# Expert sums and second-pass products of a decoder layer, alternated by four rows instead of eight, and a last block stored in halves

## The chip, the cores and the metric

The kernel runs on one core of a Trainium2 chip, all in fp32. The metric is the device time of one execution in microseconds (us). Its engines are PE (TensorE, matrix products into PSUM, which has 8 banks of 512 fp32 columns), DVE (VectorE), ACT (ScalarE), POOL (GpSimd, here only an issuer of transfers) and SP (another issuer). Transfers run on 16 DMA engines. Engines wait for one another through semaphores that the kernel sets by hand.

## The reference

One layer of a decoder for 512 prompt tokens and 8 sample tokens of width 1024:

```python
h  = rms_norm(x)*(1+sc1)+sh1            # adaLN: sh, sc, g come from c @ w_ada
q,k,v,p,ga,gb = split(h @ w_in)
A  = sliding_window_attention(q, k, v); B = multiscale_pool(p)
x  = x + g1*((sigmoid(ga)*(A@w_branch_attn) + sigmoid(gb)*(B@w_branch_pool)) @ w_out)
h2 = rms_norm(x)*(1+sc2)+sh2
x  = x + g2*PEER(h2)
```

PEER: for each of 8 heads a token's query (`h2 @ w_q`) is scored against two sets of 128 subkeys; the 16 best pairs name 16 of 16384 experts. Each expert is a row of `peer_u` and a row of `peer_v`, 1024 wide. The output is the sum over the 128 experts of a token of `gate * gelu(h2 . u_row) * v_row`.

## The kernel before

**Units.** The expert part works in 32 units (`UNITS`): block `b` of 128 tokens (four blocks) times one head. A unit has 16 U rows and 16 V rows; a "row" here is one indirect transfer by POOL (L543) that fetches one table row for each of the 128 tokens, 512 KB. A place of its own among the units, number 27 (`SAMPLES_AT`), serves the 8 sample tokens with 8 + 8 rows. That makes 520 U and 520 V gathers. U rows land in a ring of 6 buffers, V rows in another; from place 18 on (`MORE_UNIT`) each ring has 4 more.

**The order on POOL.** Its queue is written out by hand: for each place `p` and quarter `q` first four V rows of place `p - 2`, then four U rows of place `p`. A U gather waits until DVE has used the row that its buffer held (`u_used`), a V gather, at every second row, until PE has used the pair (`v_used`). What waits holds back all behind it.

**DVE** takes a dot product of each U row with the tokens (`dots`, L1121), scores and picks experts of later units between them (`route_unit`), and writes for each unit two sets of diagonal matrices (`coefficients`, L1135, `diag_ready`), eight rows each. **PE** adds the V rows into PSUM banks 0 to 3 (`combine`, L1531): a pair of rows takes 16 instructions of 64 x 64 tiles, and its end frees the pair (`v_used`). When the 8 units of a block are done, DVE scales the four banks with `g2` (`scale_sums`, L1149, `sums_scaled`), PE folds the halves and adds the transposed `x` (`fold`, L1557 and L1560, into banks 4 and 5), ACT copies the result to SBUF (`rows_out`, L740), and SP stores it (L493). Before a block's first sum PE waits until the four banks of the block before are scaled.

**Second pass.** The first part of the layer is computed for blocks 0 and 1 before the gathers begin; for blocks 2 and 3 and the sample tokens it is done beside the gathers, in steps `k` that all engines count alike: step `k` belongs to place `k // 4`, quarter `k % 4`. On PE that is `late_products(k)`: gate and A products in k = 8 to 15, gate and B in 16 to 23, the output product in 26 to 33, the transposed subkeys at 36, the mean square at 37, the token rows at `AT_H2N` (L1443), and from `AT_PQ` on one query product a step with its subkey scores (L1227, L1471, L1474). DVE (`late_work`) and ACT (`late_evacuations`) take the results; DVE normalizes at k = 39 (L854 to L870, then a memset at L1039 that raises `h_ready`), just before the scaling of block 0's sums at the start of place 10. These products use banks 4 to 7 in the order of `bank_plan`, in which the folded rows of block 0 stand as `("rows", 0, h)`. Their weights come by SP in chunks of 2 MB, in three buffers; a chunk is loaded once the last product from its buffer's chunk before is done.

PE's main loop runs over half places: two steps of products, then the eight V rows of half `f`.

```python
for n in range(2 * PLACES):
    p, f = n // 2 + 2, n % 2
    for k in (2 * n + 8, 2 * n + 9):
        late_products(k)
    ...
    combine(unit_at(p - 2), f)
    if n % 16 == 1 and 16 < n < 56:
        fold(n // 16 - 1)
```

Of the kernel before, what the change touches and what calls it, by code (L numbers as in the profile page):

```python
# [40 lines left out]
PH = 8  # L41
# [11 lines left out]
MORE_UNIT = 18  # L53
SAMPLES_AT = 27
PLACES = UNITS + 1
AT_A, AT_B, AT_O2, AT_SK, AT_SS, AT_MEAN, AT_NORM, AT_H2N, AT_PQ = 8, 16, 26, 36, 37, 38, 39, 41, 42
HW = 64


# [52 lines left out]
def bank_plan():  # L112
# [52 lines left out]
    for m in range(17):  # L165
        plan += [(("pq", m, 1), "A")] if m < 16 else []
        for i in score_tiles(m):
            plan += [(("sc", i, 1), "A"), (("scs", i), "A")]
        if m == 1:
            plan += [(("rows", 0, h), "A") for h in both]  # L170
    return plan

# [37 lines left out]
def decoder_layer(nc, x_prompt, x_sample, cache_k, cache_v, state_pool, c_prompt, c_sample, norm1_g,  # L210
# [204 lines left out]
    def unit_at(p):  # L415
        return p if p < SAMPLES_AT else p - 1
# [24 lines left out]
    def _(sp):  # L441
# [46 lines left out]
        for b in range(NB):  # L488
            if b == NB - 1:
                sp.wait_ge(sample_y_ready, 1)  # L490
                sp.dma_start(y_sample[:, 0, :], g2s_rows[0:S, :]).then_inc(sample_y_stored, 16)
            sp.wait_ge(y_ready, b + 1)
            sp.dma_start(y_prompt[0, b * P:(b + 1) * P, :], y_rows).then_inc(y_stored, 16)  # L493
        sp.wait_ge(y_stored, 16 * NB)
        sp.wait_ge(sample_y_stored, 16)

    def slot_rounds(i):
# [88 lines left out]
    def _(act):  # L586
# [143 lines left out]
        def rows_out(b):  # L730
            out = y_rows.rearrange("p (a b) -> p a b", a=2)
            if b == 0:
                for h in range(2):
                    copy(("rows", 0, h), out[:, h, :], bank(("rows", 0, h)))
                act.wait_ge(emptied_by_act, turn[("rows", 0, 1)])
                act.nop().then_inc(y_ready, 1)
                return
            act.wait_ge(rows_folded, b)
            act.wait_ge(y_stored, 16 * b)
            act.activation(out, psum[:, 4:6, :], ACT.Copy).then_inc(y_ready, 1)  # L740

        def query_scores(m, h):
            if 2 <= m < 16:
# [81 lines left out]
    def _(dve):  # L825
# [316 lines left out]
        def scale_sums(b):  # L1142

            dve.wait_ge(v_used, row(PH * b + PH - 1, TOPK))
            if b:
                dve.wait_ge(y_ready, b)
            for i in range(4):
                h = slice(i % 2 * 512, (i % 2 + 1) * 512)
                dve.tensor_tensor(scaled[i], psum[:, i, :].rearrange("p (a b) -> p a b", a=2), g2b[:, h].rearrange("p (a b) -> p a b", a=2), ALU.mult).then_inc(sums_scaled, 1)  # L1149

# [58 lines left out]
    def _(pe):  # L1209
# [300 lines left out]
            if AT_PQ <= k <= AT_PQ + 16:  # L1510
                query_scores(k - AT_PQ, 1)

        def combine(u, f):
            b, n = u // PH, 2 * u + f
            if n % 16 == 0:
                if b:
                    pe.wait_ge(sums_scaled, 4 * b)
                else:
                    for i in range(4):
                        wait_emptied(pe, plan[max(j for j in range(len(plan)) if bank_of[j] == i)][0])  # L1520
            pe.wait_ge(diag_ready, n + 1)
            for k in range(0, 8, 2):
                first, last = n % 16 == 0 and k == 0, n % 16 == 15 and k == 6
                pair = [row(u, 8 * f + k + i) for i in range(2)]
                for r in pair:
                    pe.wait_ge(v_landed[v_buf[r]], v_landing[r])
                for h in range(2):
                    for g in range(2):
                        ps = slice(g * HW, (g + 1) * HW)
                        for i, r in enumerate(pair):  # L1530
                            ins = pe.matmul(psum[i * HW:(i + 1) * HW, 2 * g + h, :], diags[n % 4][ps, k + i, :],  # L1531
                                            v_rows[v_buf[r]][ps, h * 512:(h + 1) * 512],
                                            start=first, stop=last, skip_group_check=True)
                ins.then_inc(v_used, 2)

        def combine_samples(f):
            pe.wait_ge(sample_coef_ready, 1)
            pe.wait_ge(sample_h_used, 2 * S)
            for t in range(4 * f, 4 * f + 4):
                r = sample_row(t)  # L1540
                pe.wait_ge(v_landed[v_buf[r]], v_landing[r])
                for h in range(2):
                    ins = pe.matmul(psum[0:S, 6 + h, :], coef_s[:, t * S:(t + 1) * S], v_rows[v_buf[r]][:, h * 512:(h + 1) * 512],
                                    start=(t == 0), stop=(t == S - 1), skip_group_check=True)
                ins.then_inc(v_used, 1)
            if f:
                pe.wait_ge(v_used, sample_row(S))
                pe.nop().then_inc(sample_out_ready, 2)

        def fold(b):  # L1550
            pe.wait_ge(sums_scaled, 4 * (b + 1))
            if b > 1:
                pe.wait_ge(y_ready, b)
            for h in range(2):
                o = begin(("rows", 0, h)) if b == 0 else psum[:, 4 + h, :]
                for g in range(2):
                    pe.matmul(o.rearrange("p (a b) -> p a b", a=2), halves_on[:, (1 - g) * HW:(3 - g) * HW], scaled[2 * g + h],  # L1557
                              start=(g == 0), stop=False, skip_group_check=True)
                for c in range(4):
                    ins = pe.matmul(o[:, c * P:(c + 1) * P], xT[:, 4 * h + c, cols(b)], ident,  # L1560
                                    start=False, stop=(c == 3), skip_group_check=True)
                if b == 0:
                    end(ins)
            if b:
                ins.then_inc(rows_folded, 1)

        def pick_rows(first, end_t):
            for t in range(first, end_t):
# [5 lines left out]
                    pe.matmul(psum[:, 6 + h, :], pick_s[:, t, :], h2n[NB][:, h * 512:(h + 1) * 512],  # L1574
                              start=True, stop=True).then_inc(sample_h_ready, 1)

        for n in range(2 * PLACES):
            p, f = n // 2 + 2, n % 2
            for k in (2 * n + 8, 2 * n + 9):
                late_products(k)  # L1580
            if 2 * n + 8 == AT_PQ + 18:
                for key, _ in plan[-BANKS:]:
                    wait_emptied(pe, key)
            if (p, f) == (SAMPLES_AT - 1, 1):
                pick_rows(0, 4)
            if (p, f) == (SAMPLES_AT, 1):
                pick_rows(4, S)
            if p - 2 == SAMPLES_AT:
                combine_samples(f)
            else:  # L1590
                combine(unit_at(p - 2), f)
            if n % 16 == 1 and 16 < n < 56:
                fold(n // 16 - 1)
            if (p, f) == (23, 1):
                pe.wait_ge(sample_spread, 2)
                for i in range(2):
                    ins = pe.matmul(psum[:, 6, i * S:(i + 1) * S], hs_spread[0:PH * S, i, :], kc[0:PH * S, K_SEQ:K_SEQ + S], start=True, stop=True)
                ins.then_inc(sample_turned, 1)
            if (p, f) == (SAMPLES_AT - 2, 0):
                pe.wait_ge(sample_routed, 1)  # L1600
                for i, (src, first) in enumerate(((xT, T), (mods[:, 40:48, :], 1))):
                    if i:
# [34 lines left out]
```

## Time and profile before

| | us |
|---|---|
| median of 3 runs (lowest, highest) | 1910.24 (1908.02, 1910.49) |
| the profiled execution: its own time | 1913.8 |
| its span, first to last instruction | 1911.9 |
| PE busy | 1327.0 (69%) |
| DVE busy | 1108.7 (58%) |
| POOL busy | 1108.0 (58%) |
| ACT busy | 258.6 (14%) |

The page of the profile gives busy time by engine, then 40 slices of the span, the transfers by queue, and the chain of work that ended last. A busy PE is not a PE at its peak: its clock has two levels and the page's mean granted clock is 0.82 of the full one. In views of windows, "DMA share" is the mean busy share of the 16 DMA engines; it can read a little over 1. In timelines, the bracket behind an instruction is the idle time of its engine in front of it and what ended that.

### The profile page before, as it was taken

To read this page: it belongs to the slowest core of one execution; us is meant where nothing else is said; L and a number is where in the kernel's file an instruction comes from. 1 tells how busy PE (TensorE), PEld (TensorE's weight loads), DVE (VectorE), ACT (ScalarE), POOL (GpSimd) and SP (SyncE) were. 2 spreads that over 40 slices of the span, in tenths; PEclk is the share of its full clock that TensorE was granted. 3 is DMA by queue.
4 is the path that set the end of the run, shared out by engine and by line. 5 is a ranking of instruction groups with operands and counts; after the bars stand their busy time and mean duration, and the time that the engine had idled before them with its cause. 6 is when DMAs were issued, how large, how long until landed. Compare 5 with 4: busy or idle time off the path is not lost.

```text
span 1911.9 us, 19507 instructions
## 1 busy us (share of the span) xinstructions
PE 1327.0 (69%) x7067; PEld 672.8 (35%) x7067; DVE 1108.7 (58%) x2613; ACT 258.6 (14%) x489; POOL 1108.0 (58%) x1066
## 2 busy tenths in 40 slices
PE   5999899896778857645877655556555547764567
PEld 3547667585344423213444211111111112211122
DVE  5013331267656667767557667767777666686540
ACT  2114430221111100111111101000000011100000
POOL 1201000036766677765677777777777777777773
PEclk8999897798799978788889876676667788777769
DMA  9334143869999999997999999999999999999996
GB/s 329 109 100 148 60 137 110 306 244 318 374 372 403 373 399 405 400 404 277 387 371 379 389 408 397 400 377 404 355 407 407 406 405 408 408 370 362 388 409 268
DMA packets 196265, 639.21 MB, mean 334 GB/s; under 512 B 21856, under 2 KB 23188, under 8 KB 196042
## 3 DMA queue, kind: packets, MB, share of 16 engines
q0 software_dynamic: 154992, 550.65, 74.6%
q1 hardware_dynamic: 41178, 87.31, 13.1%
q8 instruction: 57, 0.93, 0.2%
q14 instruction: 38, 0.31, 0.0%
HBM read 634.09 MB, written 3.59 MB: 334 GB/s over the span
## 4 chain that ended last, share of the span: by engine, by line
POOL 36%; PE 30%; DMA 15%; issue 12%; DVE 4%; ACT 2%; SPq 0%; DVEq 0%; POOLq 0%; ACTq 0%
POOL arena L543 36%; PE psum L1227 12%; DMA arena<-in_peer_v,arena 10%; PE psum L1531 7%; PE psum L1291 5%; DMA arena<-in_peer_u,arena 3%; PE psum L1245 1%; ACT arena L591 1%; DVE arena L1121 1%; DMA arena<-in_w_ada 1%; ACT arena L643 1%; PE psum L1318 1%; DMA arena<-in_w_in 1%; PE psum L1557 0%; DMA arena<-in_x_sample 0%
## 5 line engine op out<-in xcount | busy, mean ns | idle before, releaser
L1531 PE MATMUL psum<-arena 64*64 64x512 f32 x4096 | 665.9, 800 | 489.3 <-DMA arena<-in_peer_v,arena 474.6
L1121 DVE CUSTOM_DVE_ANT_0 arena<-arena 128x1024 f32<-128x1024 f32 x520 | 635.1, 1227 | 431.1 <-DMA arena<-in_peer_u,arena 413.4
L543 POOL DMA_INDIRECT arena<-in_peer_v,arena x520 | 548.3, 1054 | 228.2 <-issue 145.0
L543 POOL DMA_INDIRECT arena<-in_peer_u,arena x520 | 533.9, 1027 | 227.7 <-issue 155.4
L1531 PEld LDWEIGHTS psum<-arena 64*64 64x64 f32 x4096 | 202.6, 179 | 931.3 <-issue 914.2
L1227 PE MATMUL psum<-arena 128*128 128x264 f32 (+3 forms) x1620 | 382.7, 394 | 15.3 <-ACT arena L591 15.0
L1227 PEld LDWEIGHTS psum<-arena 128*128 128x128 f32 (+1 forms) x1620 | 304.2, 194 | 92.3 <-issue 41.7
L591 ACT ACTIVATE arena<-psum 128x512 f32<-128x512 f32 (+9 forms) x219 | 91.7, 447 | 492.1 <-PE psum L1227 281.1
L728 ACT ACTIVATE arena<-arena 128x16 f32<-128x16 f32 x32 | 6.9, 217 | 836.6 <-DVE arena L1121 836.6
L1291 PE MATMUL psum<-arena 128*128 128x512 f32 (+3 forms) x240 | 88.5, 528 | 2.9 <-DMA arena<-in_w_in 2.9
L1291 PEld LDWEIGHTS psum<-arena 128*128 128x128 f32 (+1 forms) x240 | 40.7, 172 | 49.9 <-issue 42.9
L538 POOL DMA_DIRECT2D arena<-in_cache_v x1 | 0.5, 537 | 87.6 <-PE psum L1401 87.6
L540 POOL DMA_DIRECT2D arena<-in_consts x1 | 0.6, 589 | 78.3 <-PE psum L1436 78.3
L1121 DVE DVE_READ_ACCUMULATOR2_ANT arena<- 128x1 f32 x520 | 43.0, 83 | 0.0
L1135 DVE TENSOR_TENSOR arena<-arena 128x512 f32<-128x512 f32 x64 | 41.6, 691 | 1.1
L728 ACT ACT_TABLE_LOAD x32 | 41.1, 1283 | 0.2
L726 ACT ACT_TABLE_LOAD x31 | 39.8, 1283 | 0.5
L1046 DVE MAX8 arena<-arena 128x8 f32<-128x128 f32 (+3 forms) x99 | 29.8, 329 | 17.1 <-ACT arena L591 16.9
L523 POOL DMA_DIRECT2D arena<-arena x2 | 1.1, 544 | 61.8 <-DVE arena L911 61.8
L848 DVE TENSOR_TENSOR arena<-psum,arena 128x36 f32<-128x36 f32 x12 | 2.3, 195 | 59.5 <-PE psum L1253 59.5
L922 DVE SCALAR_TENSOR_TENSOR arena<-psum,arena 128x512 f32<-128x512 f32 (+1 forms) x16 | 9.4, 622 | 46.8 <-PE psum L1318 46.7
L1245 PE MATMUL psum<-arena 128*32 128x512 f32 x192 | 29.8, 752 | 8.5 <-DMA arena<-in_w_ada 8.5
(197 smaller groups left out, 852.0 us busy)
## 6 DMA issues: line engine op xcount, KB each, us to landing
arena<-in_w_ada SPq DMA_DIRECT2D x12, 2048.0 KB, 12.3
arena<-in_w_in SPq DMA_DIRECT2D x10, 2048.0 KB, 14.6
arena<-in_peer_wq SPq DMA_DIRECT2D x8, 2048.0 KB, 14.2
arena<-in_peer_u,arena POOLq DMA_INDIRECT x520, 6.6
arena<-in_peer_v,arena POOLq DMA_INDIRECT x520, 7.1
arena<-in_w_out SPq DMA_DIRECT2D x4, 2048.0 KB, 14.2
arena<-in_w_branch_attn SPq DMA_DIRECT2D x4, 1024.0 KB, 11.4
arena<-in_w_branch_pool SPq DMA_DIRECT2D x2, 2048.0 KB, 12.0
```

The costliest lines, as they stand in the source:

```text
L543: pool.indirect_dma_start(out=rows_to, out_offset=None, in_=table[0], in_offset=bass.IndirectOffsetOnAxis(ap=index, axis=0)).then_inc(land ...
L591: ins = act.activation(out, in_, f, **kw)
L643: act.activation(sS[b % 2][:, h, lo:], sS[b % 2][:, h, lo:], ACT.Exp, bias=nmax[:, h:h + 1], accum_out=ssum[:, h:h + 1])
L726: act.activation(v, v, ACT.Exp)
L728: act.activation(acts[:, u % 2, :], acts[:, u % 2, :], ACT.Gelu_apprx_tanh).then_inc(gelu_done, 1)
L1046: dve.max(v[:, 0:8], s)
L1121: dve.tensor_tensor_reduce(rows_r, rows_r, h, 1.0, 0.0, ALU.mult, ALU.add, total).then_inc(u_used, 1)
L1135: dve.tensor_tensor(diags[n % 4], halves_on[:, HW:2 * HW].unsqueeze(1).broadcast_to((P, 8, HW)), coefs[:, 8 * f:8 * f + 8].unsqueeze(2).br ...
L1227: ins = pe.matmul(out, a, b, start=(n == 0), stop=(n == len(pairs) - 1))
L1245: ins = pe.matmul(o[k % 4 * 32:(k % 4 + 1) * 32, :], scT[:, k, :], w[:, k, :], start=(k < 4), stop=(k >= 4), skip_group_check=True)
L1291: ins = pe.matmul(o, hT[:, k, cols(b)], wt[:, k, 0:n], start=(k == 0), stop=(k == C - 1))
L1531: ins = pe.matmul(psum[i * HW:(i + 1) * HW, 2 * g + h, :], diags[n % 4][ps, k + i, :], v_rows[v_buf[r]][ps, h * 512:(h + 1) * 512], start= ...
```

## The change

Five things change; the amount of arithmetic does not.

- PE's loop runs over steps `k`: one step of products, then four V rows of quarter `q` (before: two steps, then eight rows). What hung on a half place hangs on a quarter; the sample rows go two by two.
- The token rows move from step 41 to 42, the query products from 42 on to 43 on. The folded rows of block 0 keep their step, 43, so that they stand one query product earlier in the order of banks.
- DVE scales the four banks in the order 0, 2, 1, 3: both parts of the first column half, then both of the second.
- A fold first adds the transposed `x` to both column halves, and only then waits for the scaled sums, half by half.
- ACT copies the folded rows in halves, and for the last block each half is stored by a transfer of its own.

```diff
--- before.py
+++ after.py
@@ -53,7 +53,7 @@
 MORE_UNIT = 18
 SAMPLES_AT = 27
 PLACES = UNITS + 1
-AT_A, AT_B, AT_O2, AT_SK, AT_SS, AT_MEAN, AT_NORM, AT_H2N, AT_PQ = 8, 16, 26, 36, 37, 38, 39, 41, 42
+AT_A, AT_B, AT_O2, AT_SK, AT_SS, AT_MEAN, AT_NORM, AT_H2N, AT_PQ = 8, 16, 26, 36, 37, 38, 39, 42, 43
 HW = 64
 
 
@@ -166,7 +166,7 @@
         plan += [(("pq", m, 1), "A")] if m < 16 else []
         for i in score_tiles(m):
             plan += [(("sc", i, 1), "A"), (("scs", i), "A")]
-        if m == 1:
+        if AT_PQ + m == 43:
             plan += [(("rows", 0, h), "A") for h in both]
     return plan
 
@@ -489,9 +489,14 @@
             if b == NB - 1:
                 sp.wait_ge(sample_y_ready, 1)
                 sp.dma_start(y_sample[:, 0, :], g2s_rows[0:S, :]).then_inc(sample_y_stored, 16)
-            sp.wait_ge(y_ready, b + 1)
-            sp.dma_start(y_prompt[0, b * P:(b + 1) * P, :], y_rows).then_inc(y_stored, 16)
-        sp.wait_ge(y_stored, 16 * NB)
+            if b < NB - 1:
+                sp.wait_ge(y_ready, b + 1)
+                sp.dma_start(y_prompt[0, b * P:(b + 1) * P, :], y_rows).then_inc(y_stored, 16)
+        for h in range(2):
+            hs = slice(h * 512, (h + 1) * 512)
+            sp.wait_ge(y_ready, NB + h)
+            sp.dma_start(y_prompt[0, T - P:, hs], y_rows[:, hs]).then_inc(y_stored, 16)
+        sp.wait_ge(y_stored, 16 * (NB + 1))
         sp.wait_ge(sample_y_stored, 16)
 
     def slot_rounds(i):
@@ -735,9 +740,12 @@
                 act.wait_ge(emptied_by_act, turn[("rows", 0, 1)])
                 act.nop().then_inc(y_ready, 1)
                 return
-            act.wait_ge(rows_folded, b)
             act.wait_ge(y_stored, 16 * b)
-            act.activation(out, psum[:, 4:6, :], ACT.Copy).then_inc(y_ready, 1)
+            for h in range(2):
+                act.wait_ge(rows_folded, 2 * b - 1 + h)
+                ins = act.activation(out[:, h, :], psum[:, 4 + h, :], ACT.Copy)
+                if h or b == NB - 1:
+                    ins.then_inc(y_ready, 1)
 
         def query_scores(m, h):
             if 2 <= m < 16:
@@ -1144,7 +1152,7 @@
             dve.wait_ge(v_used, row(PH * b + PH - 1, TOPK))
             if b:
                 dve.wait_ge(y_ready, b)
-            for i in range(4):
+            for i in (0, 2, 1, 3):
                 h = slice(i % 2 * 512, (i % 2 + 1) * 512)
                 dve.tensor_tensor(scaled[i], psum[:, i, :].rearrange("p (a b) -> p a b", a=2), g2b[:, h].rearrange("p (a b) -> p a b", a=2), ALU.mult).then_inc(sums_scaled, 1)
 
@@ -1510,59 +1518,60 @@
             if AT_PQ <= k <= AT_PQ + 16:
                 query_scores(k - AT_PQ, 1)
 
-        def combine(u, f):
-            b, n = u // PH, 2 * u + f
-            if n % 16 == 0:
+        def combine(u, q):
+            b, n, v = u // PH, 2 * u + q // 2, 4 * u + q
+            if v % 32 == 0:
                 if b:
                     pe.wait_ge(sums_scaled, 4 * b)
                 else:
                     for i in range(4):
                         wait_emptied(pe, plan[max(j for j in range(len(plan)) if bank_of[j] == i)][0])
             pe.wait_ge(diag_ready, n + 1)
-            for k in range(0, 8, 2):
-                first, last = n % 16 == 0 and k == 0, n % 16 == 15 and k == 6
-                pair = [row(u, 8 * f + k + i) for i in range(2)]
+            for k in (0, 2):
+                first, last = v % 32 == 0 and k == 0, v % 32 == 31 and k == 2
+                pair = [row(u, GS * q + k + i) for i in range(2)]
                 for r in pair:
                     pe.wait_ge(v_landed[v_buf[r]], v_landing[r])
                 for h in range(2):
                     for g in range(2):
                         ps = slice(g * HW, (g + 1) * HW)
                         for i, r in enumerate(pair):
-                            ins = pe.matmul(psum[i * HW:(i + 1) * HW, 2 * g + h, :], diags[n % 4][ps, k + i, :],
+                            ins = pe.matmul(psum[i * HW:(i + 1) * HW, 2 * g + h, :], diags[n % 4][ps, q % 2 * GS + k + i, :],
                                             v_rows[v_buf[r]][ps, h * 512:(h + 1) * 512],
                                             start=first, stop=last, skip_group_check=True)
                 ins.then_inc(v_used, 2)
 
-        def combine_samples(f):
+        def combine_samples(q):
             pe.wait_ge(sample_coef_ready, 1)
             pe.wait_ge(sample_h_used, 2 * S)
-            for t in range(4 * f, 4 * f + 4):
+            for t in (2 * q, 2 * q + 1):
                 r = sample_row(t)
                 pe.wait_ge(v_landed[v_buf[r]], v_landing[r])
                 for h in range(2):
                     ins = pe.matmul(psum[0:S, 6 + h, :], coef_s[:, t * S:(t + 1) * S], v_rows[v_buf[r]][:, h * 512:(h + 1) * 512],
                                     start=(t == 0), stop=(t == S - 1), skip_group_check=True)
                 ins.then_inc(v_used, 1)
-            if f:
+            if q == 3:
                 pe.wait_ge(v_used, sample_row(S))
                 pe.nop().then_inc(sample_out_ready, 2)
 
         def fold(b):
-            pe.wait_ge(sums_scaled, 4 * (b + 1))
             if b > 1:
                 pe.wait_ge(y_ready, b)
+            o = [begin(("rows", 0, h)) if b == 0 else psum[:, 4 + h, :] for h in range(2)]
             for h in range(2):
-                o = begin(("rows", 0, h)) if b == 0 else psum[:, 4 + h, :]
+                for c in range(4):
+                    pe.matmul(o[h][:, c * P:(c + 1) * P], xT[:, 4 * h + c, cols(b)], ident,
+                              start=(c == 0), stop=False, skip_group_check=True)
+            for h in range(2):
+                pe.wait_ge(sums_scaled, 4 * b + 2 * h + 2)
                 for g in range(2):
-                    pe.matmul(o.rearrange("p (a b) -> p a b", a=2), halves_on[:, (1 - g) * HW:(3 - g) * HW], scaled[2 * g + h],
-                              start=(g == 0), stop=False, skip_group_check=True)
-                for c in range(4):
-                    ins = pe.matmul(o[:, c * P:(c + 1) * P], xT[:, 4 * h + c, cols(b)], ident,
-                                    start=False, stop=(c == 3), skip_group_check=True)
+                    ins = pe.matmul(o[h].rearrange("p (a b) -> p a b", a=2), halves_on[:, (1 - g) * HW:(3 - g) * HW], scaled[2 * g + h],
+                                    start=False, stop=(g == 1), skip_group_check=True)
                 if b == 0:
                     end(ins)
-            if b:
-                ins.then_inc(rows_folded, 1)
+                else:
+                    ins.then_inc(rows_folded, 1)
 
         def pick_rows(first, end_t):
             for t in range(first, end_t):
@@ -1574,29 +1583,28 @@
                     pe.matmul(psum[:, 6 + h, :], pick_s[:, t, :], h2n[NB][:, h * 512:(h + 1) * 512],
                               start=True, stop=True).then_inc(sample_h_ready, 1)
 
-        for n in range(2 * PLACES):
-            p, f = n // 2 + 2, n % 2
-            for k in (2 * n + 8, 2 * n + 9):
-                late_products(k)
-            if 2 * n + 8 == AT_PQ + 18:
+        for k in range(8, 4 * PLACES + 8):
+            p, q = divmod(k, 4)
+            late_products(k)
+            if k == AT_PQ + 18:
                 for key, _ in plan[-BANKS:]:
                     wait_emptied(pe, key)
-            if (p, f) == (SAMPLES_AT - 1, 1):
+            if (p, q) == (SAMPLES_AT - 1, 2):
                 pick_rows(0, 4)
-            if (p, f) == (SAMPLES_AT, 1):
+            if (p, q) == (SAMPLES_AT, 2):
                 pick_rows(4, S)
             if p - 2 == SAMPLES_AT:
-                combine_samples(f)
+                combine_samples(q)
             else:
-                combine(unit_at(p - 2), f)
-            if n % 16 == 1 and 16 < n < 56:
-                fold(n // 16 - 1)
-            if (p, f) == (23, 1):
+                combine(unit_at(p - 2), q)
+            if q == 3 and p % PH == 2 and PH < p < 28:
+                fold(p // PH - 1)
+            if (p, q) == (23, 3):
                 pe.wait_ge(sample_spread, 2)
                 for i in range(2):
                     ins = pe.matmul(psum[:, 6, i * S:(i + 1) * S], hs_spread[0:PH * S, i, :], kc[0:PH * S, K_SEQ:K_SEQ + S], start=True, stop=True)
                 ins.then_inc(sample_turned, 1)
-            if (p, f) == (SAMPLES_AT - 2, 0):
+            if (p, q) == (SAMPLES_AT - 2, 0):
                 pe.wait_ge(sample_routed, 1)
                 for i, (src, first) in enumerate(((xT, T), (mods[:, 40:48, :], 1))):
                     if i:
```

## Rows read from the trace of the kernel before

**Rows 1.** The page: the chain by line, and the transfers by queue.

```profile
POOL arena L543 36%; PE psum L1227 12%; DMA arena<-in_peer_v,arena 10%; PE psum L1531 7%; PE psum L1291 5%; DMA arena<-in_peer_u,arena 3%; PE psum L1245 1%; ACT arena L591 1%; DVE arena L1121 1%; DMA arena<-in_w_ada 1%; ACT arena L643 1%; PE psum L1318 1%; DMA arena<-in_w_in 1%; PE psum L1557 0%; DMA arena<-in_x_sample 0%
...
q0 software_dynamic: 154992, 550.65, 74.6%
```

**Rows 2.** Windows by stage: length, busy us by engine, PE clock, DMA share, GB/s.

```profile
470.00:660.00 190.00, 143.46 (x779) 82.04 (x780) 122.41 (x298) 20.41 (x33) 130.81 (x123) 0.87 0.99 379
660.00:855.00 195.00, 122.69 (x709) 53.79 (x711) 135.08 (x336) 19.70 (x32) 139.53 (x136) 0.80 1.03 402
855.00:905.00 50.00, 28.28 (x188) 15.80 (x180) 35.87 (x84) 10.79 (x19) 28.48 (x27) 0.82 0.76 284
905.00:1080.00 175.00, 137.07 (x794) 75.66 (x798) 108.71 (x265) 23.02 (x55) 124.26 (x120) 0.88 0.99 378
```

**Rows 3.** Waits of PE and POOL, 470 to 860 us: total, times, longest.

```profile
PE psum L1531 <- DMA arena<-in_peer_v,arena: 118.0, 27, 12.0
...
POOL arena L543 <- PE psum L1531: 42.5, 20, 5.8
```

**Rows 4.** Timeline of PE and POOL: start, length, instructions, idle time before.

```profile
495.80 10.96 PE L1227 MATMUL psum<-arena 128*128 128x264 f32 x48
...
539.89 1.95 PE L1531 MATMUL psum<-arena 64*64 64x512 f32 x16 [2.42 <-DMA arena<-in_peer_v,arena]
...
627.26 10.96 PE L1227 MATMUL psum<-arena 128*128 128x264 f32 x48
638.15 3.67 PE L1531 MATMUL psum<-arena 64*64 64x512 f32 x32
...
640.40 0.97 POOL L543 DMA_INDIRECT arena<-in_peer_v,arena  x1 [5.32 <-PE psum L1531]
...
673.74 3.69 PE L1531 MATMUL psum<-arena 64*64 64x512 f32 x16 [3.90 <-DMA arena<-in_peer_v,arena]
```

**Rows 5.** Windows around three of POOL's stalls (columns as in rows 2).

```profile
536.00:542.00 6.00, 3.42 (x32) 0.91 (x24) 5.71 (x19) 0.00 (x0) 4.81 (x4) 1.00 0.79 262
638.00:650.00 12.00, 8.85 (x66) 2.59 (x65) 7.16 (x23) 0.00 (x0) 7.47 (x8) 0.90 0.81 278
...
953.00:966.00 13.00, 8.77 (x65) 2.60 (x64) 6.53 (x16) 3.16 (x5) 8.61 (x8) 0.83 0.80 267
```

**Rows 6.** Timeline at the second normalization: DVE, PE and POOL.

```profile
873.91 2.43 DVE L1149 TENSOR_TENSOR arena<-psum,arena 128x512 f32<-128x512 f32 x4
...
874.06 5.38 PE L1443 MATMUL psum<-arena 128*128 128x128 f32 x24 [16.22 <-DVE arena L1039]
...
879.37 5.55 PE L1531 MATMUL psum<-arena 64*64 64x512 f32 x48
...
881.79 1.21 POOL L543 DMA_INDIRECT arena<-in_peer_v,arena  x1 [13.90 <-PE psum L1531]
```

**Rows 7.** Timeline of the query steps: fold 0 on PE, and a stall of POOL.

```profile
914.91 1.99 PE L1557 MATMUL psum<-arena 128*128 128x512 f32 x4
...
955.25 1.78 POOL L543 DMA_INDIRECT arena<-in_peer_v,arena  x1 [4.75 <-PE psum L1531]
```

**Rows 8.** Timeline of the tail, all engines.

```profile
1898.34 2.49 DVE L1149 TENSOR_TENSOR arena<-psum,arena 128x512 f32<-128x512 f32 x4 [39.57 <-PE psum L1531]
...
1900.88 3.39 PE L1557 MATMUL psum<-arena 128*128 128x512 f32 x4 [2.60 <-DVE arena L1149]
...
1904.11 1.05 PE L1560 MATMUL psum<-arena 128*128 128x128 f32 x8
...
1905.00 1.88 PE L1557 MATMUL psum<-arena 128*128 128x512 f32 x4
...
1907.81 1.03 ACT L740 ACTIVATE arena<-psum 128x1024 f32<-128x1024 f32 x1 [51.05 <-PE psum L1560]
1908.87 0.35 SPq L493 DMA_DIRECT2D out<-arena  x1
```

**Rows 9.** Transfers issued in 555 to 600 us: count, size, us to landing.

```profile
arena<-in_w_branch_pool SPq DMA_DIRECT2D x1, 2048.0 KB, 14.7
```

## The prediction

> **What bounds the kernel now.** I read the page's chain first, then the transfers, then windows by stage, then single waits. The chain that ended last is 36% POOL and 15% DMA: it runs through the gathers of L543 [rows 1]. Their queue moves 550.65 MB in 1040 gathers, so 0.529 MB each. In 660–855 us the 16 DMA engines show a share of 1.03 at 402 GB/s, which is what this kernel reaches when they never pause; in 470–660 the share is 0.99, in 855–905 it is 0.76, in 905–1080 it is 0.99 [rows 2]. Time in which nothing moved is length × (1 − share/1.03): 190 × 0.039 = 7.4 us, 50 × 0.262 = 13.1 us, 175 × 0.039 = 6.8 us. So from the first gather on the transfers are the limit, and a change of order on PE can win only these pauses, 27.3 us together, and the tail after the last gather.
>
> Who makes the pauses? PE waits 118.0 us for second-pass rows between 470 and 860, so it has time to spare on average; yet POOL waits 42.5 us in 20 waits for PE in the same stretch [rows 3]. Both hold because of bursts: PE does two steps of products (48 matmuls, 10.96 us), then eight V rows, of which the first two pairs, already there, take 3.67 us [rows 4]. While it multiplies it frees no V buffer; there are six, POOL's queue is in order, and so the U gathers wait too. At 640.40 POOL had stood 5.32 us until the sums behind the products of 627.26 freed a pair [rows 4]. Around that stall the DMA share is 0.81 over 12 us, around another of the kind 0.79 over 6 us [rows 5]. Elsewhere in this stretch the same stall is covered by weights in flight.
>
> **The change, part by part.** The sum is made against the profiled execution, 1913.8 us (span 1911.9 us and 1.9 us around it); the median of the runs shown is 1910.24 us, 3.56 us less, and I carry the gain over to it.
>
> *Alternating by one step and four rows.* No instruction is added; 5.48 us of products (10.96/2) and 3.67 us of sums now follow each other, 9.15 us a step. A step takes (627.26 − 495.80)/10 = 13.1 us [rows 4], so PE keeps its slack, and the longest stretch without freeing a buffer halves. A stall of 5.32 us at 10.96 us of products is covered at 5.48 us. Gain at 470–660: at least 0, at most 7.4 us (all of its pauses). I take the two pauses that are visibly this stall, 6 × (1 − 0.79/1.03) + 12 × (1 − 0.81/1.03) = 1.4 + 2.6 = 4.0 us [rows 5]. The same stall at 955.25 (4.75 us of POOL, [rows 7]) has a share of 0.80 over 13 us [rows 5]: 2.9 us, bounds 0 and the stage's 6.8 us. In 660–855 there is no pause to win: 0, and since nothing pauses there, at worst a stall like the 5.32 us above. A product of an odd step now stands behind four V rows, up to 3.67 us and their landing later; DVE, which takes it, waited in 470–860 for nothing but rows (no wait on PE stands in its waits there), and POOL's order brings it those rows after PE's; I take 0, at worst 3.67 us at one place.
>
> One weight chunk gets less time: `wb` is loaded into the buffer of `wa`, free when the last A product (k = 15) is done, and needed one step later. It landed 14.7 us after its issue [rows 9]; PE now comes to it after four rows and a gate product, as little as 3.67 + 3.65 = 7.3 us later (the gate product is 16 of the 48 matmuls, 10.96/3), so PE may stand up to 7.4 us once. During that the transfers are busy with that very chunk: price 0, at worst 7.4 − 5.48 = 1.9 us.
>
> *Query products and token rows one step later.* This moves the token-row transposes (L1443) behind the first four rows of unit 8. Now PE stands until the second normalization is done, transposes 5.38 us from 874.06, and only at 879.37 adds the rows that free a buffer; POOL, idle for 13.90 us, goes on at 881.79 [rows 6]. DVE's four scalings end at 873.91 + 2.43 = 876.34, and these are all that the rows of unit 8 need. After the change the first pair runs from 876.34. At the lower clock it takes 3.69 us as after 3.90 us of waiting, at the upper 1.95 us as after 2.42 us [rows 4]. POOL goes on at 880.0 or 878.3, so 1.8 or 3.5 us earlier. PE has stood for 16.2 us there (idle in front of L1443), so the nearest row is the lower clock: 1.8 us. Nothing is won below 0, as the scalings come after the normalization on DVE anyway. The transposes move into the wait for the next gathered rows. The step that follows fold 0 waits for ACT's copies of the folded rows in the banks it reuses; before, a later step did so. Price 0, at worst as the 4.75 us stall.
>
> *Tail.* The last V sum ends near 1898.3; four scalings take 2.49 us; then PE folds: 3.39 + 1.05 + 1.88 + 1.05 us with gaps, ACT copies 1.03 us from 1907.81, and the store is issued at 1908.87 [rows 8]. After: the transposes of x (2 × 1.05 us) stand in front of the wait and run beside the scalings, to 1900.4. Two scalings, now those of the first half, are done at 1899.6, the others at 1900.83. The first half folds to 1902.3 and the second to 1904.2 (1.88 us each), its copy is half as wide (I take 0.6 us for 1.03), so the last store is issued at 1904.85 instead of 1908.87: 4.0 us. PE no longer stands in front of the fold, as in fold 0, where the same four matmuls took 1.99 us [rows 7], not the 3.39 us after the idle time of [rows 8]. The store of 512 KB ran from 1908.87 to the span's end, 3.0 us; half the bytes save at most half, at least 0: I take 0.5 us. Tail: 4.5 us; at the lower clock for one half 1.5 us less, so 3.0 to 5.5.
>
> The Trainium skill (DMA: Bandwidth & Descriptors, Anatomy of one DMA) gives each transfer about 2.0 us that do not depend on size, plus bytes at 436 GB/s. By it, as an estimate, 256 KB saves 0.6 us of a store's 3.2 us, near the 3.0 us of the trace; if the two halves paid their fixed part one after the other, the tail would win 2.5 us.
>
> *Sum:* 4.0 + 2.9 + 1.8 + 4.5 = 13.2 us, so 1900.6 us for an execution such as the profiled one and 1910.24 − 13.2 = **1897.0 us**.
>
> **Rivals.**
> 1. *The transfers hide it* (16%). POOL's stalls go, but the pauses come back at another gather, since a gather costs POOL 1.25 us with its gap and the transfers 0.529 MB/402 GB/s = 1.32 us: a lost backlog is regained by 0.07 us per gather only. For it: most stalls of POOL now cost no transfer time. Against: four measured pauses stand right behind a stall. Left is the tail: 1905.7 us (1904.7 to 1907.2).
> 2. *All goes* (12%): every pause of 470–660 and 905–1080, the upper clock at unit 8, the whole tail: 7.4 + 6.8 + 3.5 + 4.7 = 22.4 us, 1887.8 us.
> 3. *Slower by the change of array shape* (5%). Products use the array whole (128*128), sums in quarters (64*64). The change doubles the passages between them: some 23 pairs of steps are split, 46 more passages. In the rows none is to be seen: sums start at 638.15, 0.07 us before the modelled end of the products (627.26 + 10.96) [rows 4]. The place is each of the 43 steps; it decides from (13.1 − 9.15)/2 = 2.0 us a passage, when a step no longer fits. At 2.5 us a passage, the steps cost 43 × 1 = 43 us and nothing but the tail is won: 1949 us. The Trainium skill (TensorEngine Tiling (Array Packing), Key Properties) says that changing the tiling mode drains the engine, and names no price; by it this is what speaks against the change, and these rows show none.
> 4. *Slower by the clock* (4%). The granted clock is 0.87 in 470–660 [rows 2]. If shorter bursts left PE at the lower of its two levels (1.2 instead of 2.4 GHz) for over 43% of a step's work (13.1/9.15 − 1), PE would be the limit; at 60% a step costs 1.5 us, 43 steps 66 us: 1910.2 − 4.5 + 66 = 1972 us. Against: the waits get shorter, and pairs after short waits ran at the upper level [rows 4].
> 5. *Half done* (3%): the late `wb`, the copies behind fold 0 and a displaced stall take 1.9 + 4.75 + 5.32 = 12.0 us of it back: 1909 us.
>
> **How the numbers follow.** The forecast has 60%, with its own range of 1892 to 1903 us; the rivals 16, 12, 5, 4 and 3%. About 0.2% (3.8 us) can be told from no change here. Faster by more: 60 + 12 + 10 of rival 1 = 82%. Within: 6 of rival 1 and rival 5, 9%. Slower: 9%. The range from rival 2 to the poor end of rival 1, 1887.5 to 1907.2 us, leaves out rivals 3 to 5, 12%, and some of the edges.
>
> **What would show it.** Right: POOL's waits for L1531 in 470–860 fall from 42.5 us to under 15; the share in 470–660 and 905–1080 rises to 1.01 or more; POOL's stop at the normalization shrinks from 13.90 to about 12 us; from the last V sum to the last store's issue 6.5 us instead of 10.5, with no PE wait over 0.3 us in front of the fold. Wrong: POOL's waits gone but the shares unchanged (rival 1); gaps of PE at each passage (rival 3); a granted clock under 0.75 in 470–660 (rival 4); a wait of PE on a weight chunk at k = 16 or for ACT after fold 0 (rival 5).

## The result and the profile after

Before and after ran in turn on one chip: 1909.33 us before (median of 4), 1886.54 us after (1883.07 to 1887.77), ratio 0.9875 with a 95% interval of 0.986 to 0.9891. That is 22.8 us, where 13.2 were forecast; the time lies below the stated range by 1 us. In two later groups, beside other runs of before, the ratio was 0.989 (0.9861 to 0.9919) and 0.9867 (0.9839 to 0.9895), and the medians were 21.0 and 23.6 us apart.

The windows by stage of the kernel after, columns as in [rows 2]:

```profile
470.00:660.00 190.00, 154.38 (x872) 89.10 (x872) 127.28 (x307) 23.42 (x36) 138.63 (x129) 0.91 1.02 394
660.00:855.00 195.00, 114.87 (x662) 49.95 (x658) 134.32 (x335) 19.27 (x31) 143.00 (x133) 0.81 1.02 399
855.00:905.00 50.00, 29.39 (x188) 14.31 (x189) 36.13 (x86) 6.32 (x10) 29.28 (x29) 0.80 0.79 295
905.00:1080.00 175.00, 138.30 (x845) 76.65 (x847) 114.61 (x279) 27.66 (x65) 131.64 (x128) 0.94 1.02 403
```

Read the last column against [rows 2]: 379 became 394 GB/s in 470–660 and 378 became 403 in the query steps. The clock rose too (0.87 to 0.91, 0.88 to 0.94). The share beside it rose only from 0.99 to 1.02: 3%, where the rate rose by 4.0 and 6.6%. The same microseconds hold slightly different work in two kernels, so stages are compared between the same gathers further down.

Four rows from the timeline of PE show the new alternation, to be read beside [rows 4]: 5.6 us of products, then each pair as it lands, after 1.25 and 1.46 us of waiting. The products run as fast as before, 5.61 us for 24 matmuls where 48 took 10.96 us.

```profile
502.41 5.61 PE L1235 MATMUL psum<-arena 128*128 128x264 f32 x24
509.28 1.95 PE L1539 MATMUL psum<-arena 64*64 64x512 f32 x16 [1.25 <-DMA arena<-in_peer_v,arena]
512.68 1.95 PE L1539 MATMUL psum<-arena 64*64 64x512 f32 x16 [1.46 <-DMA arena<-in_peer_v,arena]
514.56 5.61 PE L1235 MATMUL psum<-arena 128*128 128x264 f32 x24
```

POOL's waits for PE in 470–860 (total, times, longest), against 42.5 us in [rows 3]:

```profile
POOL arena L548 <- PE psum L1539: 30.9, 23, 5.3
```

The longest is the one that the prediction placed: PE waits for the late `wb` chunk at step 16.

```profile
561.58 3.83 PE L1235 MATMUL psum<-arena 128*128 128x264 f32 x16
571.53 3.59 PE L1235 MATMUL psum<-arena 128*128 128x264 f32 x8 [6.12 <-DMA arena<-in_w_branch_pool]
...
577.30 0.94 POOL L548 DMA_INDIRECT arena<-in_peer_v,arena  x1 [5.34 <-PE psum L1539]
```

It cost no transfer time: neither the window over PE's wait nor the one over POOL's wait behind it falls below a share of 1.02 or 402 GB/s.

```profile
562.00:572.00 10.00, 3.88 (x17) 3.03 (x16) 5.58 (x14) 1.89 (x3) 7.83 (x8) 0.79 1.02 404
572.00:582.00 10.00, 9.49 (x52) 5.41 (x52) 3.07 (x7) 0.00 (x0) 3.78 (x4) 0.87 1.03 402
```

The second normalization, against [rows 6]: it starts at 854.84 (L862), the first sums of unit 8 follow DVE's scaling behind it, the token rows (L1451) come later, and POOL's stop is 12.50 instead of 13.90 us.

```profile
854.84 1.80 DVE L862 RECIPROCAL arena<-arena 128x264 f32<-128x264 f32 x1
...
863.61 2.42 DVE L1157 TENSOR_TENSOR arena<-psum,arena 128x512 f32<-128x512 f32 x4
866.08 8.12 PE L1539 MATMUL psum<-arena 64*64 64x512 f32 x48 [17.16 <-DVE arena L1157]
870.07 1.34 POOL L548 DMA_INDIRECT arena<-in_peer_v,arena  x1 [12.50 <-PE psum L1539]
...
879.88 3.80 PE L1451 MATMUL psum<-arena 128*128 128x128 f32 x24
```

The tail, against [rows 8]: the 16 transposes of x follow the last sums at once, beside the scaling, and the fold runs at the upper clock (3.60 us for eight matmuls). ACT ends at 1883.21, 6.05 us after the end of the last V sum (1875.21 + 1.95); before, with the last V sum in the row below, it was 10.55 us.

```profile
1896.34 1.95 PE L1531 MATMUL psum<-arena 64*64 64x512 f32 x16 [0.55 <-DMA arena<-in_peer_v,arena]
```

After:

```profile
1875.21 1.95 PE L1539 MATMUL psum<-arena 64*64 64x512 f32 x16 [0.54 <-DMA arena<-in_peer_v,arena]
...
1877.09 2.05 PE L1564 MATMUL psum<-arena 128*128 128x128 f32 x16
1877.22 2.48 DVE L1157 TENSOR_TENSOR arena<-psum,arena 128x512 f32<-128x512 f32 x4 [40.31 <-PE psum L1539]
...
1878.98 3.60 PE L1569 MATMUL psum<-arena 128*128 128x512 f32 x8
...
1880.96 0.60 ACT L746 ACTIVATE arena<-psum 128x512 f32<-128x512 f32 x1 [46.05 <-PE psum L1569]
...
1881.58 1.99 SPq L498 DMA_DIRECT2D out<-arena  x2
...
1882.61 0.60 ACT L746 ACTIVATE arena<-psum 128x512 f32<-128x512 f32 x1 [1.06 <-PE psum L1569]
```

The first gather starts anywhere from 393 to 404 us in the profiles of this study, whether or not a kernel is changed there. So stages are compared below by the starts of gathers in each trace: the first gather, then the first V gather in the turn of places 2, 10, 11, 15 and 19 (gathers 33, 289, 321, 449, 577), the last gather, the end of the span. Lengths in us, one profile each; "tail" runs from the start of the last gather to the end, and the 70 to 72 us ahead of place 2 stand in the last column alone:

```
kernel                 places 2-10  10-11  11-15  15-19  19-last  tail  first gather to end
before                    384.2      57.5  187.2  171.7   617.0   23.8     1511.1
after                     378.2      54.9  176.8  174.1   616.5   18.4     1488.3
after, second group       375.7      53.5  177.1  173.8   616.6   18.9     1485.7
after, third group        376.4      55.9  179.7  175.4   607.6   18.0     1482.5
e1 loop only              379.4      55.9  176.5  172.8   613.7   22.0     1490.6
e2 shift only             388.1      55.3  192.1  171.8   611.1   21.8     1510.0
e3 tail only              389.6      55.5  188.5  172.0   612.5   18.9     1505.9
e5 bursts to step 37      386.4      53.1  179.0  174.6   615.4   18.3     1495.8
e6 bursts from step 42    378.5      55.3  193.2  172.3   609.3   18.9     1497.3
e7 loop and tail          378.9      54.3  178.0  171.2   617.5   19.2     1489.3
e4 normalization later    376.4      48.3  176.5  173.6   615.4   17.9     1478.9
e9 the same again         377.5      48.2  177.9  173.3   614.2   18.8     1480.1
e8 pairs                  376.6      50.2  179.8  174.4   614.0   18.0     1482.9
```

### The profile page after: what moved, and what is told of

The parts are those of the page before. It is cut to its first block, busy times and chain, and to the rows that moved or that the text cites. A ratio compares the mean times of both kernels' runs of the same rounds, so it can differ in the third digit from the quotient of the medians.

```text
span 1885.7 us, 19511 instructions
## 1 busy us (share of the span) xinstructions
PE 1301.2 (69%) x7067; PEld 661.3 (35%) x7067; DVE 1108.4 (59%) x2613; ACT 257.9 (14%) x492; POOL 1113.2 (59%) x1066
## 3 DMA queue, kind: packets, MB, share of 16 engines
q1 hardware_dynamic: 41322, 87.31, 13.2%
## 4 chain that ended last, share of the span: by engine, by line
POOL 42%; PE 23%; DMA 16%; issue 14%; DVE 3%; ACT 2%; SPq 0%; DVEq 0%; POOLq 0%; ACTq 0%
POOL arena L548 42%; DMA arena<-in_peer_v,arena 11%; PE psum L1235 8%; PE psum L1539 5%; PE psum L1299 5%; DMA arena<-in_peer_u,arena 3%; ACT arena L596 1%; PE psum L1253 1%; DMA arena<-in_w_ada 1%; DMA arena<-in_w_in 1%; DVE arena L1129 1%; ACT arena L648 1%; PE psum L1326 1%; DMA arena<-in_x_sample 0%; PE psum L1583 0%
## 5 line engine op out<-in xcount | busy, mean ns | idle before, releaser
L1539 PE MATMUL psum<-arena 64*64 64x512 f32 x4096 | 647.6, 776 | 504.2 <-DMA arena<-in_peer_v,arena 454.6
L548 POOL DMA_INDIRECT arena<-in_peer_u,arena x520 | 541.2, 1041 | 223.3 <-issue 155.1
L596 ACT ACTIVATE arena<-psum 128x256 f32<-128x256 f32 (+9 forms) x219 | 90.8, 447 | 528.1 <-PE psum L1235 317.9
## 6 DMA issues: line engine op xcount, KB each, us to landing
arena<-in_w_in SPq DMA_DIRECT2D x10, 2048.0 KB, 13.6
```

What stands on the lines that cost most here:

```text
L548: pool.indirect_dma_start(out=rows_to, out_offset=None, in_=table[0], in_offset=bass.IndirectOffsetOnAxis(ap=index, axis=0)).then_inc(land ...
L596: ins = act.activation(out, in_, f, **kw)
```

## The experiments

Theory A: PE's bursts of two steps starve the V buffers, and what that costs is read from the transfer rate. Rival B: the query steps gain because they stand one step later. The first group splits the change into its parts and adds one new edit.

**e1, the loop alone** (in short, against the kernel before).

```diff
-        for n in range(2 * PLACES):        # two steps, then combine(u, f): eight rows
+        for k in range(8, 4 * PLACES + 8): # one step, then combine(u, q): four rows
```

> Of the change only the loop of one step and four V rows; steps 41 and 42 stay for token rows and query products, fold, scaling order and store are as before. Theory A (PE's bursts of two steps starve the V buffers, and the loss is what the transfer rate shows, not the pauses in the DMA share): the loop carries about 7 us in steps 8 to 33 and about 10 us in the query steps, so 15 to 18 us faster than before; GB/s in 470-660 about 394 and in the query steps about 400. Rival B (the query steps gain because query products and token rows stand one step later): 6 to 9 us faster, GB/s in the query steps still under 385.

Measured: 1886.59 us against 1907.98 us before, ratio 0.988 (0.9845 to 0.9915). The rates are those of the whole change; windows 470–660 and 905–1080:

```profile
470.00:660.00 190.00, 156.61 (x872) 89.52 (x872) 125.58 (x304) 23.41 (x36) 138.08 (x129) 0.91 1.01 394
905.00:1080.00 175.00, 130.98 (x817) 72.00 (x819) 113.57 (x275) 25.55 (x59) 127.97 (x127) 0.93 1.02 405
```

The gain, 21 us by medians, is over A's 15 to 18, though the interval (16 to 30 us) reaches into it. B falls: without the shift the query steps reach 405 GB/s.

**e2, the shift alone** (in short; the folded rows and the last wait for the banks are set to match).

```diff
-AT_H2N, AT_PQ = 41, 42
+AT_H2N, AT_PQ = 42, 43
```

> Of the change only token rows and query products one step later, in the old loop of two steps and eight rows. Theory A: at most 3 us faster (the stop at the normalization), or no difference that can be told; the query steps stay under 385 GB/s. Rival B: 8 to 12 us faster.

Measured: ratio 1.0026 (0.9999 to 1.0052), nothing that can be told from no change. The query steps are as slow as before:

```profile
905.00:1080.00 175.00, 134.12 (x796) 74.73 (x800) 106.70 (x262) 23.48 (x57) 126.61 (x116) 0.89 0.98 371
```

**e3, the tail alone** (in short).

```diff
-            for i in range(4):         # scale_sums
+            for i in (0, 2, 1, 3):
-            act.activation(out, psum[:, 4:6, :], ACT.Copy)
+            for h in range(2): act.activation(out[:, h, :], psum[:, 4 + h, :], ACT.Copy)
 ...                                    # fold: x first; SP: two stores for the last block
```

> Of the change only the fold with the transposed x first, the scaling order and the last block stored in halves. Both theories: 4.5 to 5.5 us faster, all of it behind the last gather; 10.5 us from the last V sum to the last store's issue become about 6.

Measured: 1903.83 us, ratio 0.9971 (0.9944 to 0.9998), 4.2 us by medians. Behind the last gather it has 18.9 us where before has 23.8: 4.9 us. But e1 and e2, which have the old tail, have 22.0 and 21.8 us there; see the tail below.

**e4, the whole change with the normalization behind the scaling.** The rows above show PE waiting 17.16 us for DVE, which normalizes (step 39) and only then scales block 0's sums.

```diff
-AT_NORM, AT_H2N, AT_PQ = 39, 42, 43
+AT_NORM, AT_H2N, AT_PQ = 40, 42, 43
```

> The whole change, and the second normalization one step later (40 for 39), so that DVE scales block 0's sums before it normalizes and PE's first sums of unit 8 no longer wait for the normalization. If POOL's stop of 12.5 us there is PE waiting for DVE's scaling: the stop falls under 5 us and the kernel is 4 to 9 us faster than the whole change (1878 to 1883 us). If DVE's time for the normalization (8.9 us) is what counts, since it holds up the dot products as well, the stop moves to the U buffers and the time stays within 2 us of the whole change.

Measured: 1881.85 us, ratio 0.9861 (0.9824 to 0.9898); the whole change did not run in this group. POOL's stop is 3.83 us, and DVE's reciprocal (L862), the start of the normalization, stands behind the scaling:

```profile
857.71 2.48 DVE L1157 TENSOR_TENSOR arena<-psum,arena 128x512 f32<-128x512 f32 x4
...
860.24 8.05 PE L1539 MATMUL psum<-arena 64*64 64x512 f32 x48 [7.87 <-DVE arena L1157]
...
864.23 1.48 POOL L548 DMA_INDIRECT arena<-in_peer_v,arena  x1 [3.83 <-PE psum L1539]
...
868.47 1.80 DVE L862 RECIPROCAL arena<-arena 128x264 f32<-128x264 f32 x1
```

The second group puts the bursts back in one stage at a time, and takes the shift out.

> The whole change, unaltered, beside the others of this group: 1883 to 1888 us; its profile from the first gather to the end 1488 us, as before.

Measured: 1887.73 us, ratio 0.989, and 1485.7 us from the first gather.

**e5 and e6, bursts in one stage.** The whole change, with

```diff
+            if k < 38:                 # e5; e6: if k >= 42
+                for i in (k, k + 1) if q % 2 == 0 else ():
+                    late_products(i)
+            else:
                 late_products(k)
```

> The whole change, but up to step 37 PE does two steps of products ahead of eight V rows again. Theory A (each stage gains the transfer rate that its own bursts cost): 5 to 8 us slower than the whole change, GB/s in 470-660 back to 378 to 385, in the query steps still about 403. If the gain of the query steps comes from a backlog that the early steps build, the query steps fall as well and it is over 12 us slower.

> The whole change, but from step 42 on PE does two steps ahead of eight V rows again. Theory A: 8 to 13 us slower than the whole change, GB/s in the query steps back to 375 to 382, in 470-660 still about 394. By the terms of the prediction, read from pauses in the DMA share, it would be 3 us slower.

Measured: e5 1896.2 us, ratio 0.9937 (0.9917 to 0.9957), 8.5 us over the whole change in its group by medians; e6 1900.74 us, ratio 0.9945 (0.9926 to 0.9965), 13.0 us over it by medians (10.5 by the ratios). e5's interval just touches that of the whole change, e6's does not; e5 lies a little over A's 5 to 8 us, e6 at the upper end of its 8 to 13. Each loses in its own stage (table) and keeps the rate of the other. First e5, then e6, windows 470–660 and 905–1080:

```profile
470.00:660.00 190.00, 148.13 (x816) 84.50 (x816) 123.48 (x299) 23.23 (x36) 128.29 (x120) 0.88 0.99 380
905.00:1080.00 175.00, 139.03 (x856) 78.46 (x848) 115.59 (x275) 27.47 (x65) 129.65 (x125) 0.96 1.02 399
```

```profile
470.00:660.00 190.00, 148.66 (x826) 85.51 (x827) 126.86 (x307) 20.24 (x32) 138.95 (x127) 0.89 1.01 393
905.00:1080.00 175.00, 138.08 (x792) 75.87 (x796) 105.39 (x255) 23.98 (x57) 121.32 (x114) 0.86 0.97 367
```

A rival that these rows answer is the clock, which rose with the rate: in 470–660 e5 and e6 have nearly the same clock, 0.88 and 0.89, but 380 and 393 GB/s. There the rate goes with the bursts.

**e7, loop and tail without the shift** (the diff of e2 the other way round).

> The whole change without its shift of token rows and query products (41 and 42 as before). If the shift is worth the 1.8 us of the prediction: 2 us slower than the whole change. If it costs, as the sum of the single parts suggests (loop 20.6, shift 1.1, tail 5.2 us from the first gather on, against 22.7 for all): 2 to 4 us faster than the whole change.

Measured: 1883.55 us, ratio 0.987 (0.9844 to 0.9896), beside 0.989 (0.9861 to 0.9919) for the whole change: the medians say 4 us faster, the intervals overlap. That the shift gains is not shown; that it costs isn't either. In the table the kernels with the shift and single steps after it have 173 to 175 us in places 15 to 19, the others 171 to 173; why is open.

The third group sets e4's edit beside the whole change, and alternates more finely still.

> The whole change, unaltered, as the base of the two others: 1883 to 1889 us.

> The whole change with the normalization at step 40, again, beside the whole change on one chip: 4 to 8 us faster than it, all of it between the first gathers of places 10 and 11 (48 us instead of 54).

Measured: 1887.03 us for the whole change, 1879.84 us with the normalization later, ratio 0.983 (0.9803 to 0.9856) to before. The median is 7.2 us lower, places 10 to 11 take 48.2 instead of 55.9 us. The intervals of whole change and e9 still overlap, but five of the six runs of the whole change in this group are slower than all six of e9.

**e8, pairs** (e9's kernel, in short). In steps 8 to 23 PE does the gate product, one pair of rows, the A or B product, one pair.

```diff
-            late_products(k)
+            late_products(k, (0,)); combine(unit, q, (0,)); late_products(k, (1,))
 ...
-                combine(unit, q)
+                combine(unit, q, (2,))
```

> The whole change with the normalization at step 40, and in steps 8 to 23 a finer alternation: the gate product, one pair of V rows, the second product, one pair. Theory A with the V buffers as the limit: a burst of 5.5 us is already covered, so within 3 us of the kernel without it (e9). If every burst costs in proportion, 470-660 rises from 394 to 402 GB/s and it is 3 to 4 us faster than e9. Either way the passages between array shapes double again: at 0.4 us each they would show as 25 us of PE time, and as slower.

Measured: 1877.78 us, ratio 0.982 (0.9792 to 0.9848), not told from e9; 470–660 is at 396 GB/s, e9's at 398. Halving bursts of 5.5 us gains nothing more that can be told, and twice the passages between array shapes in these steps cost nothing that can be seen.

## Why the prediction was wrong

The mechanism was right: bursts on PE hold up POOL, and with it the transfers (e1, e5, e6). Two terms of the sum were less than a half and about a quarter of what they measured. The step that failed is the first one: "Time in which nothing moved is length × (1 − share/1.03)", and with it the choice of "the two pauses that are visibly this stall" as the gain. The same rows hold a second measure, the rate: 190 × (1 − 379/402) = 10.9 us and 175 × (1 − 378/402) = 10.4 us are missing, not 7.4 and 6.8, and what the alternation gave back is about that, not only the three dips of [rows 5].

- *Steps 8 to 36*: 4.0 us forecast. Places 2 to 10 take 384 to 390 us in the four profiles with bursts there, 376 to 379 us in the nine without: 9.6 us between the means; e5 says 8.5 by medians. The stated upper bound of 7.4 us was too low as well.
- *Query steps*: 2.9 us forecast, upper bound 6.8. Places 11 to 15 take 187 to 193 us with bursts and 176 to 180 without: about 12 us; e6 says 10 to 13. This is the term that missed most.
- *Normalization*: 1.8 us forecast, 1.4 us of POOL's stop measured (13.90 to 12.50), with the first pair at the lower clock as taken. But it is not the shift's alone. With one step at a time the four rows of step 40 stand ahead of the token rows at 41 anyway. Each part by itself shortens the stop as much, first e1 (loop), then e2 (shift); beside the loop the shift adds nothing here.

```profile
POOL arena L543 <- PE psum L1531: 22.3, 5, 12.5
```

```profile
POOL arena L543 <- PE psum L1531: 27.9, 8, 12.4
```

- *Tail*: 4.5 us forecast. From the end of the last V sum to the end of the span it is 13.6 us before and 8.5 after and in e3: 5.1 us. In e1 and e2, with the old tail, it is 12.2 us, which makes it 3.7. The 1.4 us between are the clock: behind the same wait of 2.60 us the first four matmuls of the fold take 3.39 us before [rows 8] and 1.98 in e1. The prediction put the slow fold down to the idle time in front of it; the same idle time stands in front of e1's fast one.

```profile
1874.24 1.98 PE L1557 MATMUL psum<-arena 128*128 128x512 f32 x4 [2.60 <-DVE arena L1149]
```

- *Store in halves*: 0.5 us taken within the tail. From ACT's end to the end of the span it is 3.1 us before and 2.5 after, so the two halves did not pay one after the other. The formula that the prediction takes from the Trainium skill (DMA: Bandwidth & Descriptors, Anatomy of one DMA) is given there for transfers that GpSimd issues, and these stores are SP's; with 3.2 and 2.6 us, as estimates, it comes near all the same.
- *Edits priced at nothing*: the `wb` wait came, 6.12 us of "up to 7.4", behind full transfers. DVE waited in 470–860 for no product, and PE behind fold 0 not for ACT.
- *Signs named ahead*: the share rose past 1.01 in both stages, and PE no longer stands in front of the last fold. But POOL's waits in 470–860 were to fall under 15 us; they fell from 42.5 to 30.9, while the rate rose. A wait of POOL alone does not say that transfers stop.

Together, less 2 us in places 15 to 19 (e7), these sizes make 25 to 26 us, where the medians of the three groups are 21.0 to 23.6 us apart. Profiles of the whole change alone differ by 6 us from the first gather to the end, so each size is good to a few microseconds only. And where the prediction says that PE waits 118.0 us for "second-pass rows", the row shows gathered V rows.

Of the rivals, 1 falls: the stages with the stalls became shorter, and from place 19 to the last gather the profiles with the old loop (611 to 617 us) lie among those with the new one (608 to 618). 3 falls with e8, 4 with the clock of 0.91 and 0.94. 5 falls: its `wb` wait came but stopped no transfer, and PE did not wait for ACT. Rival 2, every pause gone, came within a microsecond of the gain (22.4 against 22.8 us), but by luck: its sum is too small in both stages and too large at the normalization.

Why the share understates the loss can be read from the packets. This is the queue of the gathers between the same two gathers (places 11 to 15), first 187.2 us of before, then 176.8 us of after: packets, MB, and their time as a share of 16 engines.

```profile
q0 software_dynamic: 18277, 66.55, 92.7%
```

```profile
q0 software_dynamic: 18345, 66.80, 95.7%
```

One MB took 41.7 us of an engine before and 40.5 us after. Packet by packet in the traces, the median of the 4 KB packets is nearly the same (162 and 164 ns), but 309 of 16245 took over 250 ns before and 82 of 16307 after. A slow packet counts as busy. What the slow ones took beyond 164 ns is 7.4 us of all 16 engines before and 1.4 us after; the prediction's formula, with the share to three places (0.998 and 1.022), gives pauses of 5.7 and 1.3 us. The two falls, 6.0 and 4.4 us, are the 10.4 us by which the stage became shorter. With both taken off, places 11 to 15 have 173 to 175 us left in all thirteen profiles. So the formula counted less than half of that loss. Before, 64% of the slow packets lie in or next to 2 us with under 350 GB/s, which make up 30% of the stage; why they are slow no run shows.

## What to carry to other kernels

When transfers are the limit, read what a stage loses from its GB/s against the best stage of the same kernel, or from its length between the same transfers, and use the busy share only to place the loss: slow packets count as busy. A ring of buffers covers a burst on its consumer up to some length; here six V buffers did not cover 10.96 us of products, and below 5.5 us a finer alternation gained nothing that could be told. A clock read from one profile's rows can be that of the one execution: look at the same rows in a second profile before pricing it. Before moving work to another step, ask whether another part of the change already puts it there.

## Not expected

Before, 50 × (1 − 284/402) = 14.7 us of transfers are missing around the normalization, the largest single hole, and the change left 13.3 of them (295 GB/s). One number, the step of the normalization, took that window to 344 GB/s, 7.2 us missing, though DVE does the same work: about half of the hole was its order against the scaling. What the other half is due to is not shown.
